# A ring of five 4 MB weight areas in place of eight of 2 MB, in a one-core decoder layer with 32 experts

## What is computed

```python
def moe(x, w_r, b_r, w1, b1, w2, b2):              # x: 264 rows of 1024, normalised
    logits = xt.astype(F32) @ w_r.astype(F32) + b_r.astype(F32)
    top_v, top_i = lax.top_k(logits, TOP_K)         # 4 of 32 experts for each row
    gw = jax.nn.softmax(top_v, axis=-1)
    ...
    for e in range(N_EXPERTS):                      # 32
        hdn = xt @ w1[e] + b1[e]                    # w1[e]: 1024 x 2048, 8 MB
        gate = jnp.minimum(hdn[:, :D_FF_EXPERT], SWIGLU_LIMIT)
        up = jnp.clip(hdn[:, D_FF_EXPERT:], -SWIGLU_LIMIT, SWIGLU_LIMIT)
        act = (up + 1.0) * gate * jax.nn.sigmoid(SWIGLU_ALPHA * gate)
        out = out + combine[:, e:e + 1] * (act @ w2[e] + b2[e])   # w2[e]: 1024 x 1024, 4 MB
```

```python
    h = h + y @ w_out[l]
    h = h + moe(rmsnorm(h, g_ffn[l]), ...)
    gate = jax.nn.sigmoid(rmsnorm(h, g_ple[l]) @ w_pg[l] + b_pg[l])
    h = h + gate * (p[l] @ w_pp[l])                 # p[l]: 264 x 256, w_pp: 256 x 1024
```

## Time and profile before

| what | value |
|---|---|
| median of 3 runs | 1099.24 us (1096.77 to 1099.93) |
| the profiled execution's own time | 1099.61 us |
| its span, first to last instruction | 1097.9 us |
| PE busy, share of the span | 1043.5 us, 95% |
| transferred | 426.75 MB, mean 389 GB/s |
| granted TensorE clock, mean | 0.997 of full speed |

### The profile page before, as it was taken

One profiled execution on the slowest core, in us unless ns is written; L12 is line 12 of the kernel. 1 busy time (PEld: TensorE's weight loads), 2 busy tenths in 40 slices (PEclk: granted clock), 3 DMA queues, 4 the chain that ended last, 5 costly groups with the idle time before them and its releaser, 6 DMA issues.

```text
span 1097.9 us, 15991 instructions
## 1 busy us (share of the span) xinstructions
PE 1043.5 (95%) x6374; PEld 434.4 (40%) x6374; DVE 386.0 (35%) x879; ACT 153.9 (14%) x268; POOL 12.6 (1%) x20
## 2 busy tenths in 40 slices
PE   9999999999999999999999999899999999999996
PEld 7884433333333333333333333233333333333332
DVE  6563743233333333333332222233333323332236
ACT  2560600101000000000000000000000000000034
POOL 0100200000000000000000000000000000000000
PEclk9999999999999999999999999999999999999998
DMA  9955599999999999999999999999999999999941
GB/s 292 354 190 206 208 388 427 428 429 429 427 425 427 429 428 430 427 429 429 427 429 428 428 428 429 430 429 427 426 429 429 429 429 429 427 427 427 426 173 40
DMA packets 40136, 426.75 MB, mean 389 GB/s; under 512 B 6216, under 2 KB 7444, under 8 KB 15536
## 3 DMA queue, kind: packets, MB, share of 16 engines
q1 hardware_dynamic: 40112, 426.41, 93.1%
HBM read 424.57 MB, written 1.43 MB: 388 GB/s over the span
## 4 chain that ended last, share of the span: by engine, by line
PE 65%; DMA 31%; DVE 3%; issue 1%; ACT 0%; DVEq 0%; SPq 0%
DMA ring<-in_w 31%; PE bank L1593 25%; PE bank L1634 14%; PE bank L1308 5%; PE bank L1526 3%; PE bank L1396 3%; PE bank L1536 3%; PE bank L1544 2%; PE bank L1683 1%; PE bank L1692 1%; DVE h L1110 1%; PE bank L1621 1%; PE bank L1580 1%; PE bank L1242 1%; PE bank L1615 1%
## 5 line engine op out<-in xcount | busy, mean ns | idle before, releaser
L1593 PE MATMUL bank<-ring,xgT 128*64 128x512 f32 x1536 | 341.0, 594 | 22.9 <-DMA ring<-in_w 22.9
L1593 PEld LDWEIGHTS bank<-ring,xgT 128*64 128x64 f32 x1536 | 106.7, 137 | 236.3 <-issue 183.8
L1634 PE MATMUL bank<-ring,actT 128*64 128x512 f32 x768 | 170.1, 595 | 0.0
L1152 DVE TENSOR_SCALAR gmin<-bank 128x512 f32<-128x512 f32 x32 | 22.1, 692 | 377.4 <-PE bank L1593 377.4
L1146 DVE TENSOR_SCALAR wpick<-slot_no,pos,share 128x128 f32<-128x128 f32 (+1 forms) x96 | 27.1, 339 | 229.5 <-PE bank L1593 229.5
L1634 PEld LDWEIGHTS bank<-ring,actT 128*64 128x64 f32 x768 | 53.0, 137 | 116.5 <-issue 101.9
L698 ACT ACTIVATE sig<-gmin 128x512 f32<-128x512 f32 x32 | 20.1, 630 | 484.8 <-DVE gmin L1152 484.8
L1110 DVE TENSOR_TENSOR h<-bank,h 128x512 f32<-128x512 f32 x132 | 84.8, 684 | 8.4 <-PE bank L1536 7.3
L1536 PE MATMUL bank<-y,wpickT 64*128 64x512 f32 x264 | 65.6, 615 | 0.8 <-ACT y L705 0.8
L1526 PEld LDWEIGHTS bank<-pick,x_parts 128*128 128x128 bf16 x1584 | 55.9, 98 | 25.5 <-issue 24.7
L1593 PE MATMUL bank<-far,xgT 128*64 128x512 f32 x256 | 57.9, 594 | 6.2 <-DMA far<-in_w 6.2
(11 more groups left out here) (296 smaller groups left out, 724.5 us busy)
## 6 DMA issues: line engine op xcount, KB each, us to landing
ring<-in_w SPq DMA_DIRECT2D x144, 2048.0 KB, 31.0
far<-in_w SPq DMA_DIRECT2D x24, 2048.0 KB, 32.5
hn_nT<-in_w SPq DMA_DIRECT2D x24, 2048.0 KB, 31.0
ring<-in_w_in SPq DMA_DIRECT2D x3, 2048.0 KB, 11.9
ring<-in_w_out SPq DMA_DIRECT2D x1, 4096.0 KB, 15.8
ring<-in_w_pg SPq DMA_DIRECT2D x4, 1024.0 KB, 28.5
h<-in_x_prompt SPq DMA_DIRECT2D x2, 512.0 KB, 3.9
ring<-in_w_in SPq DMA_DIRECT2D x2, 512.0 KB, 7.3
```

Of the source, the lines that this page charges most:

```text
L1152: dve.tensor_scalar(gmin[:], bank[0][:], LIMIT, None, ALU.min).then_inc(gmin_ready, 1)
L1593: ins = pe.matmul(bank[part][r, :], xgT[:, k, :], w[:, c:c + HALF], start=False, stop=(k == W1_SLOTS - 1), skip_group_check=True)
L1634: ins = pe.matmul(bank[2][CAP * m:CAP * (m + 1), :], actT[:, half:half + CAP], pair[:, c:c + HALF], start=(f == 0), stop=(f == FF // P - 1 ...
```

## The change

The ring becomes five areas of 4 MB, 20 MB in place of 16, on a map of the on-chip memory that is written out by address. An area holds a *quad* of four slots: two quads of the first weight and one of the second for each expert. The first weight goes in single transfers of 4 MB, with contiguous runs of 32 KB per partition; the second in two halves of 2 MB, each with its own semaphore, with the 16 KB runs of before. Seven quads of the first weight at the start (HALVES_AT_FIRST: 0, 1, 3, 4, 6, 7, 10 in the order of all quads) and those of the last two experts go in halves too. A whole quad is refilled when all four slots of the area's old content are free, a half when its two are. With five areas the pattern repeats after five steps: five are written out, a loop of five passes repeats five, and two more are written out behind it.

For the 20 MB, other tensors share room: pw (the embedding) is kept by blocks of 128 columns over part of w_pp, so that w_pp is loaded in runs of 512 bytes and the embedding is multiplied in blocks of 128 columns; the samples' embedding is made behind step 2, transposed, and turned back in the tail by eight transposes. A run of 32 KB brings four input rows to one partition, so x_parts is gathered at every fourth column where it was every second (x_quads in place of x_pairs). The gather never stands inside the first weight's slots any more, and the last step makes none.

```diff
-    PAIRS, W1_PAIRS = SLOTS // 2, W1_SLOTS // 2
+    AREAS, FOUR, QUADS, W1_QUADS = 5, 4, SLOTS // 4, W1_SLOTS // 4
+    PERIOD = AREAS
+    LAST = NE % PERIOD
+    HALVES_AT_FIRST = (0, 1, 3, 4, 6, 7, 10)
...
-    AREAS, PERIOD = 8, 4
...
-        area = [ring[:, 2 * s:2 * s + 2, :].rearrange("p s n -> p (s n)") for s in range(SLOTS // 2)]
-        area += [hn_nT[:, 0:2 * FF2], far[:]]
+        ring = at(RING, "ring", [P, AREAS * FOUR, FF2])
+        area = [ring[:, FOUR * s:FOUR * (s + 1), :].rearrange("p s n -> p (s n)") for s in range(AREAS)]
...
+        def in_halves(g):
+
+            return g % QUADS >= W1_QUADS or g in HALVES_AT_FIRST
...
-            for j in range(W1_PAIRS - 1):
-                sp.wait_ge(z_made, NB * (j + 1))
-                load_pair(0, j, 0)
+            for g in range(3):
+                sp.wait_ge(z_made, NB * (g + 1))
+                load_quad(0, g // 2, 0, g % 2)
...
-            def freed(r, j):
-
-                return 2 * (PAIRS * r + j - AREAS) + 2
+            def refill(earlier, more, r, j, parts):
+
+                s, g = (QUADS * r + j) % AREAS, QUADS * (PERIOD * more + r) + j - AREAS
+                e = (earlier * PERIOD + (PERIOD * more + r)) % NE
+                if parts == 1:
+                    sp.wait_ge(slots_free, earlier * (PERIOD * SLOTS) + (FOUR * g + FOUR))
+                    load_quad(r, j, e)
+                else:
+                    for part in range(2):
+                        sp.wait_ge(slots_free, earlier * (PERIOD * SLOTS) + (FOUR * g + 2 * part + 2))
+                        load_quad(r, j, e, part)
...
-                            pe.matmul(dst, x_pairs[:, q, t, k // 2, :, k % 2], pick[:, t, :], start=(t == 0 and q == 0),
+                            pe.matmul(dst, x_quads[:, q, t, k // FOUR, :, k % FOUR], pick[:, t, :], start=(t == 0 and q == 0),
...
-                    if k == W1_SLOTS - 2 and phase == PERIOD - 1:
-                        gather(i + 1)
...
-                if phase < PERIOD - 1:
+                if not (tail and phase == LAST - 1):
                     gather(i + 1)
...
-            with pe.Fori(1, periods) as period:
+            with pe.Fori(1, blocks) as period:
                 for r in range(PERIOD):
                     step(period, r)
+            for r in range(LAST):
+                step(blocks, r, True)
...
+            for b in range(KD):
+                ins = pe.transpose(bank[6 + b // 4][0:NS, (b % 4) * P:(b % 4 + 1) * P], pwT_samples[:, b, :], ident[:])
+            ins.then_inc(samples_back, 1)
```

More of the change, by code:

```diff
@@ new lines, in decode_step @@
+        (h, b1_parts, y, ident, ones_b, before_b, slot_no, expert_pick, vecT, pos, share, eps_col, sumsq, squares,
+         table_junk, rms, rstd, n_steps, x_parts, xs_parts, pT, gmin, uclip, sig, actT, xgT, pick, wpick, wpickT,
+         b1_pick, top, picked_b, ex, negmax, exsum, rounds, head_sum, group_sum, pw, _) = lasting
+        GMIN, SIG, XGT, PARTS_AT, PW = [where[name] for name in ("gmin", "sig", "xgT", "x_parts", "pw")]
+        lg, left, br_row = row(PW, PW + 4 * 2 * P, ("lg", [P, NT, NE + TOP_K]), ("left", [P, NT, NE + TOP_K]),
+                               ("br_row", [P, NE]))
@@ L442, in _ @@
             sp.wait_ge(z_made, 4 * NB)
[L443 to L446 removed]
+            load_quad(0, 1, 0, 1)
+            sp.wait_ge(news_ready, 1)
+            for k in range(PLE // P):
+                load(w_pp[:, :, k, :], a["w_pp"][0][k * P:(k + 1) * P, :].rearrange("p (b n) -> p b n", n=P), wpp_in)
+            sp.wait_ge(yass_made, 1)
@@ L471, in _ @@
[L471 to L480 removed]
+            sp.wait_ge(xs_h, 3)
@@ new lines, in _ @@
+            for r in range(1, PERIOD):
+                for j in range(2 if r == 1 else 0, QUADS):
+                    refill(0, 0, r, j, 2 if in_halves(QUADS * r + j) else 1)
+            sp.wait_ge(steps_ready, 1)
+            blocks = sp.value_load(n_steps[0:1, 2:3], min_val=BLOCKS[0] - 1, max_val=BLOCKS[-1] - 1)
+            with sp.Fori(0, blocks) as i:
+                for r in range(PERIOD):
+                    for j in range(QUADS):
+                        refill(i, 1, r, j, 1 if j < W1_QUADS else 2)
@@ L481, in _ @@
+            for r in range(LAST):
+                for j in range(QUADS):
+                    refill(blocks, 1, r, j, 2)
+            sp.wait_ge(slots_free, blocks * (PERIOD * SLOTS) + (PERIOD + LAST - 1) * SLOTS)
             for j in range(4):
@@ L1556, in _, with step, filled @@
             ins.then_inc(wpick_turned, 1)
-            pe.wait_ge(pw_ready, 2)
             pe.wait_ge(b2_in, 32)
             pe.wait_ge(b1_placed, 16 * 4 * PARTS)
-            def step(period, phase):
+            def step(period, phase, tail=False):
                 i = period * PERIOD + phase
-                def filled(j):
-                    s, g = (PAIRS * phase + j) % AREAS, PAIRS * phase + j
-                    pe.wait_ge(area_in[s], (period * (PERIOD * PAIRS // AREAS) + (g // AREAS + 1)) * 16)
-                    return area[s]
+                def filled(j, part):
+                    s, g = (QUADS * phase + j) % AREAS, QUADS * phase + j
+                    if type(period) is int:
+                        whole, half, halves = fills(g, False), fills(g, True), in_halves(g)
+                    else:
+                        earlier = range(s, g, AREAS)
+                        rows2 = sum(q % QUADS >= W1_QUADS for q in earlier)
+                        whole = (period - 1) * W1_QUADS + (FIRST_WHOLE[s] + len(earlier) - rows2)
+                        half = (period - 1) + (FIRST_HALF[s] + (len(earlier) if tail else rows2))
+                        halves = tail or j >= W1_QUADS
+                    if halves:
+                        pe.wait_ge(half_in[s][part], (half + 1) * 16)
+                    else:
+                        pe.wait_ge(whole_in[s], (whole + 1) * 16)
+                    return area[s][:, 2 * part * FF2:2 * (part + 1) * FF2]
                 started = type(i) is int and i == 0
```

440 lines of the change are left out of this document (210 added, 230 removed).

## The result

The changed kernel takes 1101.44 us (median of 20 runs, 1098.39 to 1103.37), the kernel before 1099.17 beside it: a ratio of 1.0024, with an interval of 1.0017 to 1.0031. By that ratio it is slower by 2.6 us (2.3 by the medians), where 8 less were forecast. The profiled execution took 1102.24 us, its span is 1100.5.

What follows compares the result with a forecast made beforehand. PE on the ring's store bounds the kernel first, full transfers from about 138 us on. -9.8 - 4.0 + 4.8 + 1.1 - 0.4 + 0.3 = -8.0 us from 1099.6 gives 1091.6, stated as 1091.5; range 1086 to 1097.

Steps and rivals of the forecast that it cites:

- Twelve steps stand written out or in a first pass where eight did ... +0.3: PE's code: six more 16 KB packets fetched beside the transfers cost 0.5 us, partly in gaps, so +0.3 us.
- The loop's code no longer stays: Rival, chance 0.18: five looped steps aren't kept on chip, four passes refetch about seven packets each; 2.2 to 2.6 us more, 1094.
- say 0.08 each: Price in us of one packet of PE's code, from 427 against 428 GB/s: 0.5 to 0.9 us for ten.
- The stalls at the loop's jump cost nothing, since PE is ahead by then: At PE's loop jumps, if code is fetched again: stalls priced at 0, as PE outpaces the transfers.
- seven packets may be kept as six were: Argument against code being refetched: the five-step loop's seven packets may stay on chip like the four-step loop's six.
- gains nothing that waits: Router stage: it loses the samples' embedding, hidden behind the picks, and gets no new waiting work; put at 0.
- Two transfers less, -9.8: At the start: ten 2 MB transfers ahead of the first refill where eight were, each worth 4.9 us; -9.8 us.
- Runs of 32 KB, -4.0: First weight's transfers: 53 whole quads save 75 ns each, at 9.4 ns a run per engine; -4.0 us.
- Late releases, +4.8: Behind steps 3 and 4: whole quads wait for four free slots, idling DMA engines 3.2 and 1.6 us; +4.8 us.
- Tail, +1.1: At the end of the tail: eight transposes come between PE's matmuls, with no cover; +1.1 us.
- The last gather's -0.4: Last step: its gather between the last two pairs goes; only about 0.4 of its 1.77 us was on the path.
- The gather at every fourth column: Rival, chance 0.05: the gather's weight loads slow down, 3.8 us a step, PE binds; about +70 us, 1170.

Runs made afterwards that it cites:

- fast version: Changed kernel with a loop of 1784 instructions, waits as padding at the start and the samples' embedding back in the router stage: 1089.89 us; without the padding 1097.67.
- padded one: Changed kernel with ten instructions less in the loop (1784) and forty waits that do no work moving it to a block border: 1094.41 us, ratio 0.9955.

## Why the prediction was wrong

**The step that failed** is "Twelve steps stand written out or in a first pass where eight did ... +0.3", with the rival "The loop's code no longer stays", which had the mechanism at a chance of 0.18 and two prices wrong. The sum put 0.3 us on the code; by the runs it cost 5 to 8. First, "say 0.08 each" was read from the mean rate, and so spreads a packet over all 16 engines. The landing times show that it sets one engine back by about 1.57 us, that half of the engines take them all, and that the slowest one decides: about 1.57 / 8 = 0.2 us a packet at the end. 42 more packets make 8.2; the distance grew from 3.7 to 11.1, by 7.4. Second, "The stalls at the loop's jump cost nothing, since PE is ahead by then": a pass of five steps has 5 x (29.4 - 26.98) = 12.1 us of slack, and the first jump took 10.5 of it. So PE, which never waited for a transfer there, came to the last half at 1037.3 by its own work, about as late as the slowest engine brought it. What the stalls would have cost with even engines was not measured by itself. The fast version with and without padding puts the two at 7.8 us, the changed kernel against the padded one at 7.0 with a start that differs; together 5 to 8. The argument "seven packets may be kept as six were" was right as far as it goes. What it left out is the position: the loop touched eight, and one more is fetched behind its end.

The Trainium skill (Runtime: NRT & Kernel Launch, Instruction fetch mechanics) has crossing a border of 16 KB mostly hidden and prefers unrolled code. The runs agree for PE, which never stood still in written-out steps, and not for the transfers beside it: written out, the kernel before lost 0.65%. The Trainium skill's 2048 instructions for PE (same section) agree with the runs: eight blocks of 256 were kept and nine were not.

**The router stage**, "gains nothing that waits" and put at 0, was wrong by 2.7 us in these two profiles: the first refill left at 140.73, 138.00 in the earlier trace rows. Chain of the changed kernel:

```profile
126.45 0.80 PE bank L1501 x6
131.37 0.68 DVE pick L1060 x3
...
137.01 13.97 PE bank L1627 x55
```

The stage ran into a half clock. That the missing embedding was the reason is refuted by the runs that put work there. The size differs between executions: the first refill left at 137.7 to 141.3 in the profiles of the changed kernel and its variants, at 138.00 and 138.95 in the two with the old ring.

**Two transfers less, -9.8**: right in the main. The DMA engines are idle from 138 us on (share 0.00 above), so all ten were in; held back in the fast version, the two cost 8.2.

**Runs of 32 KB, -4.0**: right. 3.2 by the times, 3.6 by the rates; 1215 ns for a run (median of the packets) against 613 for one of 16 KB make 11 ns a run, 9.4 forecast.

**Late releases, +4.8**: right in place and size. In the padded run the two windows above, at 208 and 369 GB/s where 430 is full, lack 3.1 and 1.4 us of transfers; 3.2 and 1.6 were forecast. From 300 to 360 us the rate is 430, so there is no third gap. 4.5 us came back when the samples' embedding left step 2. The embedding's own prices, forecast at 3.5 and 3.9, were 3.67 and 3.67 to 3.77:

```profile
217.76 3.67 PE bank L1510 x32
221.43 3.67 PE bank L1520 x32
...
252.20 3.77 PE bank L1520 x32
```

**Tail, +1.1**: 0.97 (L1731, eight transposes, in the chain at 1077.43). The last gather's -0.4 was not measured by itself.

**The gather at every fourth column**: its loads became slower, 118 ns for 98 in the earlier trace rows, six matmuls took 0.20 us for 0.18, and a step 26.98 us in place of 26.77. That is 0.21 of the 3.8 that the rival put at stake, and under the 1.5 at which it decides.

```profile
L1547 PEld LDWEIGHTS bank<-pick,x_parts 128*128 128x128 bf16 x1536 | 62.1, 118 | 25.3 <-issue 23.5 <-POOL x_parts L541 1.8
```

With the code at rest the remaining terms hold in the main: 1094.4 with the padding alone, where 1091.5 were forecast. The 1089.9 with the samples' embedding moved as well is another kernel, and does not confirm the sum. The 2.9 are not taken apart further. The padded run's start was 0.75 later in its profile, the 1.6 and 0.8 by which the two transfers and the long runs fell short point the same way, and so do its 23 packets of code, six more than before.

## What to carry to other kernels

When a change makes a loop's body longer, count its instructions and the 16 KB blocks that it touches, and the one fetched behind its end; here 1784 instructions from just behind a border fetched nothing again, and the same 1784 from 16 ahead of it cost 7.8 us. Where all DMA engines are full, price every small transfer beside them by the slowest engine, not by its bytes over 16. And two terms can cancel: the comparison of run lengths showed nothing until the idle stretch that the short runs filled had been removed.

## What the runs showed of the hardware

- A packet of code took 1.07 us on its engine (median of the changed kernel) and set it back by about 1.57, and only eight of the 16 engines fell behind by it.
- At the first jump to code that was not kept, PE stood 2.1 us for the first block and 5.8 for the next, while the transfers ran at full share (1.05); then it worked at half clock, 16.16 us for 13.73.
- In the fast version the clock also fell for 3.4 us six times from 615 to 940 us, each time within 1.4 us behind a wait of 2.0 us for a whole quad, though not behind each such wait; with halves, where PE waited 0.7 and 1.2 us in the steps of that stretch, it did not (0.98 and 1.00 in the windows of 420 to 960 us).
